# Second RWKV layer: the key projection first, four strips of it chunk by chunk, the low-rank products behind it

## The reference

```
xx = 0.5 * (prev + nxt) - h
xr, xw, xk, xv, xa, xg = [h + xx * mu[n] for n in range(6)]
r = xr @ wr                      # 1024 x 1024 each
k = xk @ wk
v = xv @ wv
lw    uses tanh(xw @ w1)         # two directions, 64 columns each
a     uses xa @ a1               # 64 columns
g     uses sigmoid(xg @ g1)      # 160 columns
```

## Time and profile before

| | us |
|---|---|
| median of 3 runs | 2782.01 |
| the profiled execution | 2779.9 |
| its span | 2777.8 |
| PE busy in it | 2348.6 (85%) |
| first matmul of the stage | 1446.10 |
| last eviction of the stage begins | 1618.56 |

### The profile page before, as it was taken

How to read it: one execution, slowest core, us unless ns; L and a number is a source line. 1 busy time by engine, 2 the same in 40 slices (tenths; PEclk the granted TensorE clock), 3 DMA queues, 4 the chain that set the end, 5 groups by cost and what they waited for, 6 DMA issues and landing times. The chain is left out here.

```text
span 2777.8 us, 41426 instructions
## 1 busy us (share of the span) xinstructions
PE 2348.6 (85%) x18063; PEld 1187.6 (43%) x18063; DVE 795.6 (29%) x1627; ACT 527.6 (19%) x1110; POOL 316.6 (11%) x480
## 2 busy tenths in 40 slices
PE   7999985679698888788859958999987988878887
PEld 3333444544443333333324437888873332222222
DVE  2005517551321111111152025777633111001101
ACT  2001214750200000000030024444421000000001
POOL 0000000620000000000041006353410000000000
PEclk9999998789799999999979978999988999999999
DMA  8656110330599999999931243323229999999997
GB/s 293 258 219 236 65 60 1 105 147 10 209 421 424 424 424 424 424 424 424 423 114 46 78 138 74 53 47 71 41 72 370 422 424 424 424 424 424 424 424 304
DMA packets 204804, 709.31 MB, mean 255 GB/s; under 512 B 90460, under 2 KB 125076, under 8 KB 148432
## 3 DMA queue, kind: packets, MB, share of 16 engines
q1 hardware_dynamic: 204096, 706.45, 65.0%
q10 hardware_dynamic: 528, 0.22, 0.0%
HBM read 689.49 MB, written 17.12 MB: 254 GB/s over the span
## 5 line engine op out<-in xcount | busy, mean ns | idle before, releaser
L1640 PE MATMUL bank<-moe_w,moe_xT 128*64 128x512 f32 (+3 forms) x2568 | 530.8, 564 | 137.9 <-DMA moe_w<-in_exp_w 137.9
L1640 PEld LDWEIGHTS bank<-moe_w,moe_xT 128*32 128x32 f32 (+1 forms) x2568 | 165.8, 123 | 500.9 <-issue 340.6
L1667 PE MATMUL bank<-moe_w,moe_hidT 128*32 128x512 f32 (+1 forms) x1166 | 272.7, 600 | 12.0 <-ACT moe_hidT L1708 9.2
L1738 DVE TENSOR_TENSOR moe_silu<-bank,moe_silu 64x512 f32<-64x512 f32 (+3 forms) x96 | 61.9, 644 | 694.3 <-ACT moe_silu L1701 694.3
L1701 ACT ACTIVATE moe_silu<-bank 64x512 f32<-64x512 f32 (+3 forms) x96 | 53.0, 553 | 984.7 <-PE bank L1640 984.7
L1751 DVE COPY moe_rows<-bank 32x512 f32<-32x512 f32 x96 | 65.8, 686 | 374.6 <-PE bank L1667 373.8
L1781 POOL TENSOR_TENSOR moe_xn<-moe_xn,moe_w 128x1024 f32<-128x1024 f32 x6 | 18.1, 3011 | 1340.9 <-ACT moe_w L1717 1340.9
L504 PE MATMUL bank<-w_slab,mixT 128*128 128x512 f32 x384 | 167.9, 595 | 1.2 <-PE bank L504 1.2
L1667 PEld LDWEIGHTS bank<-moe_w,moe_hidT 128*32 128x32 f32 (+1 forms) x1166 | 89.0, 123 | 171.0 <-issue 160.4
L1901 PE MATMUL bank<-mixture,rw_slab 128*128 128x512 f32 (+1 forms) x384 | 143.6, 527 | 4.5 <-PE bank L1901 3.7
L501 PE MATMUL bank<-mixT,w_slab 128*128 128x512 f32 x320 | 143.6, 603 | 2.5 <-DVE mixT L571 2.5
(11 more groups left out here) (491 smaller groups left out, 3066.2 us busy)
## 6 DMA issues: line engine op xcount, KB each, us to landing
moe_w<-in_exp_w SPq DMA_DIRECT2D x320, 1408.0 KB, 28.5
x_res<-in_exp_w SPq DMA_DIRECT2D x64, 1408.0 KB, 35.3
o_gate<-in_ada_w SPq DMA_DIRECT2D x27, 1024.0 KB, 6.4
w_slab<-in_ab_w_in SPq DMA_DIRECT2D x22, 1024.0 KB, 9.4
z_gate<-in_ada_w SPq DMA_DIRECT2D x13, 1024.0 KB, 6.5
mixT<-ss_rows SPq DMA_DIRECT2D x32, 256.0 KB, 3.3
x_inv_and_t<-x_blocks SPq DMA_DIRECT2D x32, 256.0 KB, 4.8
wo_slab<-in_ab_w_out SPq DMA_DIRECT2D x15, 512.0 KB, 9.8
```

Source lines behind the costliest of these rows:

```text
L1640: mm = pe.matmul(g.ps[k][64 * m:64 * m + M, 0:hi - lo], xg[:, i % 2, j, c, :], w[:, (2 * m + r) * FF + lo:(2 * m + r) * FF + hi], start=(c ...
L1667: mm = pe.matmul(g.ps[5 + m][64 * m:64 * m + M, :], hidt[:, c, :], w[:, at:at + 512], start=(c == 0), stop=(c == FC - 1))
L1738: ins = dve.tensor_tensor(hid[:, lo:hi], g.ps[k][64:64 + M, 0:hi - lo], hid[:, lo:hi], ALU.mult)
```

## The change

The order of the products becomes `k`, `w`, `a`, `g`, `v`, `r`. The first four strips of the key are no longer made one after the other: a block ahead of the loop takes each mixed chunk as it comes and does the four strips' matmuls of it, into four banks. It waits for both slabs of the ring first, and frees both at its end. SP issues the two slabs first, then the low-rank weights, then the clears. The wait for the low-rank weights moves to the second product. ACT evicts the key strips first; the point at which the key is written out follows the new count, as does the value's.

```diff
-    order = ((1, "w"), (4, "a"), (5, "g"), (2, "k"), (3, "v"), (0, "r"))
+    order = ((2, "k"), (1, "w"), (4, "a"), (5, "g"), (3, "v"), (0, "r"))
+    AHEAD = 4
...
             @block.sync
             def _(sp):
-                for d in range(2):
-                    sp.dma_start(lora[:, :, 64 * d:64 * d + 64], a["rw_w1"][0, d].rearrange("(c p) r -> p c r", p=P)).then_inc(s_lora, 16)
...
+                def lora_in():
...
                 for name in "kvr":
                     for q in range(4):
                         if n == RING:
+                            lora_in()
...
-                    sp.wait_ge(s_ev, 4 + 8 * (n + 1))
+                    sp.wait_ge(s_ev, (8, 20, 28)[n])
...
             @block.tensor
             def _(pe):
                 k = 0
-                pe.wait_ge(s_lora, 64)
+                for r in range(RING):
+                    pe.wait_ge(s_slab[r], 16)
+                for c in range(DC):
+                    pe.wait_ge(s_mix, c + 1)
+                    for q in range(AHEAD):
+                        mm = pe.matmul(g.ps[q][:, :], slab[:, q // 2, c, P * (q % 2):P * (q % 2) + P], mix[:, 0, c, :], start=(c == 0), stop=(c == DC - 1))
+                        if c == DC - 1:
+                            mm.then_inc(s_mm, 1)
+                k = AHEAD
+                pe.wait_ge(s_mm, k)
+                for r in range(RING):
+                    pe.nop().then_inc(s_free, 1)
                 for n, (m, name) in enumerate(order):
...
+                    if n == 1:
+                        pe.wait_ge(s_lora, 64)
                     for q, part in enumerate(parts):
+                        if n == 0 and q < AHEAD:
+                            continue
...
-                            ns = 4 * (n - 3) + q // 2
+                            ns = 4 * "kvr".index(name) + q // 2
```

More of the change, by code:

```diff
@@ L1803, in _ @@
             def _(sp):
-                for d in range(2):
-                    sp.dma_start(lora[:, :, 64 * d:64 * d + 64], a["rw_w1"][0, d].rearrange("(c p) r -> p c r", p=P)).then_inc(s_lora, 16)
-                sp.dma_start(lora[:, :, 128:192], a["rw_a1"][0].rearrange("(c p) r -> p c r", p=P)).then_inc(s_lora, 16)
-                sp.dma_start(lora[:, :, 192:352], a["rw_g1"][0].rearrange("(c p) r -> p c r", p=P)).then_inc(s_lora, 16)
+                def lora_in():
+                    for d in range(2):
+                        sp.dma_start(lora[:, :, 64 * d:64 * d + 64], a["rw_w1"][0, d].rearrange("(c p) r -> p c r", p=P)).then_inc(s_lora, 16)
+                    sp.dma_start(lora[:, :, 128:192], a["rw_a1"][0].rearrange("(c p) r -> p c r", p=P)).then_inc(s_lora, 16)
+                    sp.dma_start(lora[:, :, 192:352], a["rw_g1"][0].rearrange("(c p) r -> p c r", p=P)).then_inc(s_lora, 16)
                 n = 0
@@ L1914, in _, with kept @@
                         act.activation(xx[:, c, lo:hi:SEG - 1], g.hT[:, c, lo + 1:hi - 1:SEG - 3], ACT.Copy).then_inc(s_edge, 1)
-                act.wait_ge(s_mm, 1)
+                def kept(dst, q, k):
+                    act.wait_ge(s_mm, k + 1)
+                    act.activation(dst[:, q, :], g.ps[k % 8][:, 0:SEG] if dst is g.rT else g.ps[k % 8][:, :], ACT.Copy).then_inc(s_ev, 1)
+                for q in range(8):
+                    kept(g.kT, q, q)
+                act.wait_ge(s_mm, 9)
                 act.activation(g.tw[:, :], g.ps[0][:, :], ACT.Tanh).then_inc(s_ev, 1)
-                act.wait_ge(s_mm, 2)
+                act.wait_ge(s_mm, 10)
                 act.wait_ge(s_zero, 96)
                 act.activation(g.ta[0:64, :], g.ps[1][0:64, :], ACT.Copy).then_inc(s_ev, 1)
-                act.wait_ge(s_mm, 3)
+                act.wait_ge(s_mm, 11)
                 act.activation(g.tg[:, 0, :], g.ps[2][:, 0:SEG], ACT.Sigmoid).then_inc(s_ev, 1)
-                act.wait_ge(s_mm, 4)
+                act.wait_ge(s_mm, 12)
                 act.activation(g.tg[0:32, 1, :], g.ps[3][0:32, 0:SEG], ACT.Sigmoid).then_inc(s_ev, 1)
[L1924 to L1928, removed]
+                for n, dst in enumerate((g.vT, g.rT)):
+                    for q in range(8):
+                        kept(dst, q, 12 + 8 * n + q)
 def stage_rwkv(g, wo):
```

## The result

The changed kernel took 2790.06 us (median of 13 runs, 2786.08 to 2794.66), the kernel before 2783.93 us beside it (13 runs, 2778.36 to 2788.81). The ratio is 1.002, with a 95% interval of 1.0012 to 1.0027: slower by about 5.6 us (the medians lie 6.1 apart), at the very edge of what was called no change (0.2%). The forecast was +4.7 us. The profiled executions differ more, 2779.9 against 2786.1 us, because 1.6 us of it arose before the stage: SP's first issue of the stage came at 1437.34 us before and comes at 1438.94 now. So the stage is measured from this issue.

A forecast was written before the change was run, and what follows sets the result against it. The last expert mixture is bound by its weight stream, which starts behind the whole mixer, so projection-stage shifts move it. Terms sum to 58.4 us against 53.7, +4.7: median 2786.7 us, range 2781.5 to 2790.5.

The forecast's parts named there:

- PE's start: Start of the projection stage: with both key slabs first in SP's queue, PE starts 0.5 us earlier; bounds -1.1 to +2.0.
- block with one drain, at full clock: Four key strips at once: 64 passes of 0.43 us, 27.5 us, plus one remaining drain of 0.3.
- half clock at the start: First passes of the four-strip block: low clock now counts, costing 1.6 us; bounds 1.5 and 2.7.
- the new wait: Key strip 4, behind the block: PE waits for slab 2 from issue to landing, 5.6 us; bounds 5.2 and 8.8.
- half clock behind it: Work behind the wait for slab 2: clock falls to half, costing 1.8 us; bounds 0 and 2.7.
- first low-rank product: `w`, now behind the key: costs 7.2 us as `a` did, since its mixing ends while key strips still run.
- the other two: Low-rank products `a` and `g`, behind `w`: keep their 14.9 us.
- Rival 2: Slabs 2 and 3 share the DMA engines, slab 2 lands after 8.7 us: wait 8.8, +7.9, 2789.9 us; chance 0.15.
- rival 1: At key strip 4 the clock holds through the wait, only 5.6 is paid: +2.9, 2784.9 us; chance 0.12.
- Rival 3: Slab 2 in place when the four strips end, no wait: gain of 2.7 us, 2779.3; chance 0.04.
- rival 4: The shift is swallowed before the last expert stream and doesn't show at the end: 0; chance 0.06 with other shifts.

The follow-up runs named there:

- warm_fill: The fill kernel plus seven matmuls of no use at the start of PE's program, before it waits for the slabs; ratio 1.0004 to the kernel before.
- lora_first: The changed kernel with SP's old order of loads, low-rank weights first, then the two key slabs; ratio 1.0046 to the kernel before.
- ring3: The changed kernel with a third place in the slab ring, PE still waiting for the first two slabs only; ratio 0.9998 to the kernel before.
- fill: The changed kernel with six matmuls of no use behind the frees of the two slabs, while SP loads the third; ratio 1.0008 to the kernel before.
- best: The changed kernel with three ring places, slab 1 waited for only before its first matmul, and four useless matmuls at the start; 2776.69 us, ratio 0.9978.
- ahead2: The changed kernel with two strips at once instead of four, waiting only for slab 0; ratio 0.9985 to the kernel before.
- ahead0: The changed kernel without the block: key first and its slabs loaded first, strips made one after the other; ratio 0.9998 to the kernel before.
- ahead2_warm: The ahead2 kernel plus four matmuls of no use before PE waits for the first slab; ratio 0.999 to the kernel before.

## Why the prediction was right

The predicted range (2781.5 to 2790.5) holds the median, and the mechanism was the forecast's: gain in the block, a new wait for a load with nothing over it, half clock behind. The median lies only 0.4 us inside the range's upper end and 3.4 over the forecast of 2786.7. Of this, 1.9 is the base: the kernel before took 2783.93 us over 13 runs where the forecast counted from the 2782.01 of three. The other 1.4 is the difference itself, 6.1 by the medians for 4.7. That the absolute time still fell inside was partly luck. Term by term, in us:

| step | forecast | measured |
|---|---|---|
| PE's start | -0.5 | -0.6 (8.14 for 8.76) |
| block with one drain, at full clock | 27.8 | 27.75 (warm_fill, 1446.28 to SP's next issue at 1474.03) |
| half clock at the start | 1.6 | 2.55 (30.3 to SP's next issue, less 27.75) |
| the new wait | 5.6 | 5.1 |
| half clock behind it | 1.8 | 1.7 (31.07 for four strips, 29.35 before; 1.9 at the pair, less 0.15 for a drain that the kernel before had) |
| first low-rank product | 7.2 | 7.4 |
| the other two | 14.9 | 15.05 |
| sum against 53.7 | +4.7 | +5.2 |

*PE's start* was read rightly from lone loads, although slabs and low-rank loads share the queue; lora_first shows the other order, 13.62.

*Half clock at the start* was the mis-sized term: I took the kernel before's 1.6 where the changed kernel had 2.5, half of its 5.0 us at half clock. Its length differs from profile to profile: half clock lay over 2.96 us in the kernel before, 5.0 in the changed one, 3.5 in ring3, 4.3 in fill and 5.8 in lora_first (a single profile each). The bound of 2.7, from another stage, held; the central value should have lain between.

*The new wait* was sized 0.5 too long, and at 5.1 it lies just under its own lower bound of 5.2: slab 3's load queued behind slab 2 didn't stretch it. This error and the 0.9 of the start's half clock partly cancel, so the sum is nearer than its terms. Rival 2, a landing of 8.7, is out with a landing at 5.0 in the changed kernel and an idle time of only 5.09 in lora_first; the 8.7 before had the low-rank loads ahead of it. The estimate by the Trainium skill ("DMA: Bandwidth & Descriptors", "Anatomy of one DMA — SWDGE (gpsimd) path") of 4.4 us was 0.6 too short against the landing at 5.0 on this issuing path; the measured rows were the better guide.

*Half clock behind the wait*: rival 1 is out, since the clock fell in the changed kernel and in lora_first, and fill removed this part. The Trainium skill ("TensorE: Matmul & The Clock Gate", "HAM oscillation — how this bites in real kernels") says that bursts with DMA waits between them restart at half clock; by that rule the term stands, and these runs agree.

*Rival 3* (a gain with no wait) was priced at -2.7. Its condition doesn't hold in the changed kernel, with 5.20 us idle; ring3 makes it hold, and there it came to -2.2. The timing speaks against *rival 4* (nothing reaches the end): what each kernel's stretch alone would give lies inside the interval of its ratio, from best (-5.9 us, 0.21%) to lora_first (+11.3, 0.41%), and the intervals of the changed kernel, ahead2, lora_first and best leave out 1. The whole difference of the changed kernel's profile (+6.2 in the span) is 1.6 before the stage and 5.2 in it, less 0.6 behind it. This says how far one profile's span can be off: SP's first issue lies between 1436.42 and 1439.36 us in the ten profiles, with the same code ahead of it.

The chances leaned to no change (0.63) against slower (0.34) on a sum of 4.7 with a bound of 5.6. The outcome lies on that bound; nothing measured here decides between the two.

## What to carry to other kernels

Work that is merged over several buffers of a ring frees them all at once: with as many places as the merged step holds, the next load has no work over it and its whole latency is paid, with half clock behind it. Merge only as many strips as leave one buffer's work for after the merged step (two of four here), or add a place. And when a producer (DVE here) is the limit, count how many strips just cover it: 2 x 0.86 us against 2.03 was nearly enough here, and the other two strips at once cost the cover and, even with a third place, gained little (85.95 with all of best's edits, 86.98 with two strips).

## What the runs showed of the hardware

The granted clock also fell without any long idle time: in ahead0 PE was never idle for more than 0.91 us once it had started, but busy for only 3.89 of 6.83 us, and the next 3.4 us ran at half clock. The cause is inferred from this one profile; no experiment took the waits for DVE away with all else alike. Work of no use kept the clock (fill, 1.00 through the wait of 5.2 us). It costs nothing only where the engine would wait at least as long: in fill it held the restart back by 0.3 us, in ahead2_warm the start by 1.5.

Two 1 MB loads issued back to back: the first landed 5.0 us after its issue in the changed kernel, where the earlier trace rows has 5.1 and 6.1 for lone ones, and PE, waiting for both, started 8.1 us after the first issue.
